# A two-layer hybrid decoder step on Trainium2: the layer loop written out, the layer's ends run token tile by token tile, and a fourth place for expert weights

## The reference

```python
def decoder_layer(x, ...):
    h = rmsnorm(x, norm1_g)
    au, av, bq, bk, bv, cq, ck, cv, cz, cb, ca = split_cols(h @ w_in)
    out_a = chunk_mlp(au, av, ...)                     # spatial gating, 4 groups x 64
    out_b = dilated_attention_blocked(q, k_all, v_all) # 6 heads, cache of 2048 rows
    qkv, conv_state = short_conv(concat(cq, ck, cv), conv_buf, c_conv_w)
    o, s_new = gated_delta(...)                        # 6 heads, chunks of 64
    x = x + concat(out_a, out_b, out_c) @ w_out
    x = x + hier_moe(rmsnorm(x, norm2_g), w_group, w_router, w1, w3, w2)
    return x, (k_new, v_new, a_rows, conv_state, s_new)
for l in range(2): xp, xs = decoder_layer(...)         # prompt and sample
y_prompt, y_sample = rmsnorm(xp, final_g), rmsnorm(xs, final_g)
```

## Time and profile before

| what | value |
|---|---|
| median of three executions | 1950.37 us |
| profiled execution, its time | 1945.06 us |
| its span, first to last instruction | 1943.1 us |
| mean granted TensorE clock | 0.883 of full |
| PE busy | 1553.9 us (80%) |
| PEld busy | 1020.3 us (53%) |
| DVE / ACT / POOL busy | 621.2 / 400.6 / 169.7 us |
| read from HBM, written | 313.25 MB, 37.83 MB |
| weights of the experts, transfers | 192 of 1024 KB, median 18.5 us from issue to landing |

### The profile page before, as it was taken

The page is one execution under the profiler, slowest core; times in us unless marked ns, Lnnn a source line. Parts: engine busy times, 40 slices in busy tenths (PEclk is TensorE's granted clock), DMA queues, the critical chain, the costliest instruction groups (busy, mean ns, idle before and its releaser), DMA issues. The chain is left out here.

```text
span 1943.1 us, 31857 instructions
## 1 busy us (share of the span) xinstructions
PE 1553.9 (80%) x12956; PEld 1020.3 (53%) x12956; DVE 621.2 (32%) x1587; ACT 400.6 (21%) x955; POOL 169.7 (9%) x211
## 2 busy tenths in 40 slices
PE   6999978887679597878399998888785896978880
PEld 3476566765445354544155765667653454544450
DVE  2433155665113211111245322566541132111113
ACT  3221122322311111111131212223232110111111
POOL 0000000000000322222000000000000012222210
PEclk9999998895789699999799989889867897999995
DMA  7152010002862599999440511000047535999984
GB/s 274 45 177 80 1 36 2 2 18 58 226 236 79 170 390 394 397 395 401 151 143 10 189 58 35 2 2 2 20 121 223 197 124 216 387 398 394 397 336 155
DMA packets 97141, 337.13 MB, mean 174 GB/s; under 512 B 33325, under 2 KB 44941, under 8 KB 72317
## 3 DMA queue, kind: packets, MB, share of 16 engines
q1 hardware_dynamic: 77484, 307.86, 44.0%
q0 software_dynamic: 13296, 25.98, 3.9%
q10 hardware_dynamic: 6240, 1.57, 0.4%
HBM read 313.25 MB, written 37.83 MB: 181 GB/s over the span
## 5 line engine op out<-in xcount | busy, mean ns | idle before, releaser
L1587 PE MATMUL bank<-ring,proj_raw 128*64 128x256 f32 x2048 | 264.2, 411 | 79.9 <-DMA ring<-in_w 77.0
L1587 PEld LDWEIGHTS bank<-ring,proj_raw 128*64 128x64 f32 x2048 | 168.8, 143 | 156.2 <-issue 94.9
L1362 PE MATMUL bank<-ring,hT_raw 128*128 128x384 f32 (+2 forms) x768 | 229.2, 462 | 0.0
L1362 PEld LDWEIGHTS bank<-ring,hT_raw 128*128 128x128 f32 x768 | 149.0, 195 | 78.0 <-issue 4.8
L2175 DVE TENSOR_TENSOR qkv_raw<-qkv_raw,bank 128x128 f32<-128x128 f32 x64 | 18.4, 287 | 446.9 <-ACT qkv_raw L1022 446.9
L1299 PE MATMUL bank<-hT_raw,ring 128*128 128x512 f32 x288 | 127.6, 596 | 0.0
L1608 PE MATMUL bank<-ring,proj_raw 128*64 128x512 f32 x512 | 123.9, 604 | 1.5 <-issue 1.5
L1507 PE MATMUL bank<-ring,hT_raw 128*128 128x512 f32 x256 | 113.6, 597 | 0.0
L1080 PE MATMUL bank<-work 64*64 64x64 f32 (+1 forms) x1608 | 73.1, 256 | 37.6 <-DVE work L1730 26.2
L1574 PE MATMUL bank<-consts,proj_raw 64*128 64x64 f32 x512 | 70.1, 278 | 29.0 <-DMA proj_raw<-h_rows,idx 29.0
L1080 PEld LDWEIGHTS bank<-work 64*64 64x64 f32 (+1 forms) x1608 | 66.7, 168 | 47.0 <-DVE work L1730 29.5
(11 more groups left out here) (312 smaller groups left out, 1988.8 us busy)
## 6 DMA issues: line engine op xcount, KB each, us to landing
ring<-in_w SPq DMA_DIRECT2D x192, 1024.0 KB, 18.5
ring<-in_w_in SPq DMA_DIRECT2D x10, 1536.0 KB, 15.1
ring<-in_cache_win_k SPq DMA_DIRECT2D x16, 768.0 KB, 8.7
ring<-in_cache_win_v SPq DMA_DIRECT2D x16, 768.0 KB, 13.7
ring<-in_cache_win_k SPq DMA_DIRECT2D x16, 576.0 KB, 6.9
ring<-in_cache_win_v SPq DMA_DIRECT2D x16, 576.0 KB, 11.1
ring<-in_w_out SPq DMA_DIRECT2D x4, 2048.0 KB, 11.7
h_rows<-proj_raw SPq DMA_DIRECT2D x16, 512.0 KB, 3.6
```

Of the source, the lines that this page charges most:

```text
L1362: mm = pe.matmul(bank[0:ROWS[t], 0:w.shape[2]], hT[:, k, 128 * t:128 * t + ROWS[t]], w[:, k, :], start=k == 0, stop=k == KT - 1)
L1587: mm = pe.matmul(bank[CAP * j:CAP * j + CAP, 0:256].rearrange("p (w f) -> p w f", w=2), rowsT[k % 2][:, CAP * c:CAP * c + CAP], w13[:, :, ...
```

## The change

The loop over layers becomes plain code, twice. Semaphores are no longer cleared: each layer has its own set (`class Signals`), or the count goes on from layer to layer. The meeting of the engines at a layer's end goes. TensorE, before it enters the second layer, waits only for the banks of the experts.

Expert weights get a fourth place, in columns of `work` and of the projection buffer `proj_raw` that hold nothing any more once the output projection begins. Expert 1 takes it, then every fourth; the ring's slots go to experts 0, 2, 3 and every fourth after each. Its first load waits for `mix_ready` and for the end of `mixT` instead of for a part of `w_out`, and stands ahead of the first four `h2_store` pairs. The expert loops of TensorE, ScalarE and VectorE take twelve experts a turn, two turns, with eight experts written out; SP's takes four.

At the ends, adding the results, the squares, the root, the scaling and (after layer 1) the final multiplication run tile by tile in a pipeline, `enter`, over ScalarE and VectorE. The next layer's gain and loads 1 and 2 are issued when `down` of experts 28 and 30 is done; load 0 is issued behind the ten reads of `y_rows`; conv state and taps behind that, when the first tile has been added (they go to columns that `got` uses). `final_g` is loaded behind the last expert's weights. The outputs are stored tile by tile. `hst` moves to the end of `qkv_raw`.

```diff
-        hst = [qkv_raw[:, D * i:D * i + D] for i in range(2)]
+        hst = [qkv_raw[:, D * (3 + i):D * (3 + i) + D] for i in range(2)]
-        EUN = 6
+        EUN = 12
+        def up_home(e):
+            slot = (E_AT, None, E_AT + 1, E_AT + 2)[e % 4]
+            return work[:, 0:4096] if slot is None else ring[:, slot % 3 * SLOT:slot % 3 * SLOT + 4096]
+        def down_home(e):
+            slot = (E_AT, None, E_AT + 1, E_AT + 2)[e % 4]
+            return proj_raw[:, 8192:10240] if slot is None else ring[:, slot % 3 * SLOT + 4096:slot % 3 * SLOT + 6144]
 # SP
-            with sp.Fori(0, DEPTH) as L:
+            gain_load(0)
+            conv_loads(0)
+            for n in range(3):
+                stream(0, n, loads[n](0, n))
+            for L in range(DEPTH):
...
-                for e in range(3):
-                    sp.wait_ge(*used_up(E_AT + e - 3))
-                    up_load(e, (E_AT + e) % 3)
-                    down_load(e, (E_AT + e) % 3)
-                    for i in ((0, 1, 2, 3), (), (4,))[e]:
+                for e in range(4):
+                    if e == 1:
+                        sp.wait_ge(s.mix_ready, 1)
+                    else:
+                        sp.wait_ge(*used_up(E_AT + (0, None, 1, 2)[e] - 3))
+                    up_load(e, e)
+                    if e == 1:
+                        sp.wait_ge(s.act_filled, A_AT[("mixT", NT - 1, 1)] + 1)
+                        sp.wait_ge(pool_stored, (L + 1) * (16 * STORES))
+                    down_load(e, e)
+                    for i in ((), (0, 1, 2, 3), (), (4,))[e]:
                         h2_store(i)
...
+                if L + 1 < DEPTH:
+                    gain_load(L + 1)
+                    for n, e in ((1, NE - 4), (2, NE - 2)):
+                        sp.wait_ge(s.act_filled, A0 + 2 * e + 2)
+                        stream(L + 1, n, loads[n](L + 1, n))
+                else:
+                    sp.dma_start(g_final, ins["final_g"][None, :].broadcast_to([128, D])).then_inc(fin_gain, 16)
...
-                leave_layer(sp, L)
+                if L + 1 < DEPTH:
+                    stream(L + 1, 0, loads[0](L + 1, 0))
+                    sp.wait_ge(got_used, L * NT + 1)
+                    conv_loads(L + 1)
+            for t in range(NT):
+                sp.wait_ge(fin_row, t + 1)
+                if t < NP:
+                    sp.dma_start(outs["y_prompt"].rearrange("b (t p) d -> t p (b d)", p=128)[t], x[:, t, :]).then_inc(y_stored, 16)
+                else:
...
 # ScalarE
+            def enter(L):
+                for t in range(NT + 1):
+                    if t < NT:
+                        if L:
+                            act.wait_ge(got_used, (L - 1) * NT + t + 1)
...
+                        act.activation(junk1[0:ROWS[t]], x[0:ROWS[t], t, :], ACT.Square, accum_out=ssq[0:ROWS[t], t:t + 1]).then_inc(row_squared, 1)
+                    if t >= 1:
+                        u = t - 1
+                        act.wait_ge(row_asked, L * NT + u + 1)
+                        act.activation(rstd[:, u:u + 1], rstd[:, u:u + 1], ACT.Sqrt).then_inc(row_root, 1)
+                        if L < DEPTH:
...
+                            act.activation(hst[u % 2][0:ROWS[u]], x[0:ROWS[u], u, :], ACT.Copy,
+                                           scale=rstd[0:ROWS[u], u:u + 1]).then_inc(of_layer[L].rows_ready, 1)
 # VectorE (joined: the two additions of tile t; asked_root: mean, EPS, reciprocal)
+            def enter(L, normed):
+                for t in range(NT + 2):
+                    if L and t < NT:
+                        joined(L - 1, t)
+                    if 1 <= t <= NT:
+                        asked_root(L, t - 1)
+                    if t >= 2:
+                        normed(t - 2)
```

More of the change, by code:

```diff
@@ L495, in build @@
+        of_layer = [Signals(L) for L in range(DEPTH)]
         a_jobs, v_jobs = schedule()
@@ L721, in _ @@
-                sp.sem_inc(aside, 1)
+                    sp.wait_ge(rows_stored[k], 16 * (L + 1) * per_buffer[k] + 16)
                 for t in range(NT):
@@ L840, in _ @@
+            for L in range(DEPTH):
+                s = of_layer[L]
+                steps, roots, asked = [0], [0], [0]
+                enter(L)
                 bank = get(("tapsT",))
-                act.activation(taps, bank[:, 0:NCT * 28].rearrange("p (c n) -> p c n", c=NCT), ACT.Copy).then_inc(act_drained, 1)
+                act.activation(taps, bank[:, 0:NCT * 28].rearrange("p (c n) -> p c n", c=NCT), ACT.Copy).then_inc(s.act_drained, 1)
                 for i in range(NCT + 1):
@@ L1261, in _ @@
             pe.wait_ge(consts_loaded, 16)
-            with pe.Fori(0, DEPTH) as L:
-                pe.wait_ge(taps_loaded, 32)
+            for L in range(DEPTH):
+                s = of_layer[L]
+                if L:
+                    pe.wait_ge(of_layer[L - 1].act_drained, A0 + 2 * NE)
+                    pe.wait_ge(of_layer[L - 1].vec_drained, V0 + 2 * NE)
+                pe.wait_ge(taps_loaded, L * 32 + 32)
                 bank, done = job(("tapsT",))
@@ L1405, in _ @@
                 for t in range(NT):
-                    delta_tile(pe, L, t, job, after, tr, lambda point, t=t: side(t, point) if t < NP else None)
+                    delta_tile(pe, s, t, job, after, tr, lambda point, t=t: side(t, point) if t < NP else None)
                 def cached(n, b):
@@ new lines, in inv_root, with step_done, joined @@
+                dve.wait_ge(s.root_ready, roots[0])
+            def step_done(ins):
+                counted[0] += 1
+                ins.then_inc(row_step, 1)
+                dve.wait_ge(row_step, counted[0])
+            def joined(L, t):
+                r = ROWS[t]
+                for k in range(2):
+                    j = 2 * t + k
+                    dve.wait_ge(gathered[j], L * 16 + 16)
+                    w = (w0, w1_)[k][0:r, place(t):place(t) + 1]
+                    ins = dve.scalar_tensor_tensor(x[0:r, t, :], got[j][0:r, :], w, x[0:r, t, :], ALU.mult, ALU.add)
+                    if k == 0:
+                        step_done(ins)
+                    else:
+                        ins.then_inc(got_used, 1)
@@ L1927, in _ @@
             groups = ((128, slice(0, NP), NP), (NS, slice(NP, NT), 1))
-            with dve.Fori(0, DEPTH) as L:
-                dve.wait_ge(first_squares, NT)
-                norm_scale()
-                dve.sem_inc(norm_asked, 1)
-                dve.wait_ge(gain_loaded, 16)
+            for L in range(DEPTH):
+                s = of_layer[L]
+                steps, roots = [0], [0]
                 def gained(label, t, h, gain):
```

752 lines of the change are left out of this document (355 added, 397 removed).

## The result

The changed kernel takes 1923.82 us (median of four executions, 1920.01 to 1926.24), the kernel before on the same chip 1951.08 us (1949.14 to 1954.27). The ratio is 0.986 with a 95% interval of 0.984 to 0.989: faster, by 27 us or 1.4%, where 26 us were predicted. On a second chip the same pair gave 1916.25 against 1948.15, ratio 0.984 (0.979 to 0.989).

The account below looks back on a forecast made before the run. The expert stage was taken to be bound by weight transfers at 390 GB/s. Terms of -16.2, -11, 0 and +1 summed to -26.2 us, taking the median from 1950.4 to 1924; range 1911 to 1938, with about 2 in 10 outside.

Parts of the forecast that it names:

- A: Expert stages: the fourth place leaves 28 experts' weights to load after `up(0)`; -16.2 us for both layers, bounds 0 and -18.
- C: End of the program: tile-by-tile work hides under the reads and the stores get smaller; -11 us, bounds -7 and -13.
- B: Layer 0 to layer 1: earlier `tapsT` wins 1.5 us, TensorE's lower clock may lose 3; 0 us, bounds -8 and +6.
- S: Start of the program: squares and single roots now stand between ScalarE's copies; +1 us, bounds -2 and +3.
- R2: Layer boundary: taps land early and TensorE keeps its clock, so B gives -8 us; 1916 us, chance 17%.
- The rest: Constants for loop counters, some `aside` increments gone, longer expert turns: 0 us, bounds -3 and +1.
- R1: Expert stages: the fourth place gives no time, leaving 1940 us; chance 8%.
- R3: Expert loops: instruction fetches of the longer turns stall TensorE; priced at +45 us, 1995 us, chance 5%.
- R4: Prefetch or pipeline waits for a semaphore reached only at the old place; A and C halve, 1937 us, chance 2%.

Follow-up runs that it names:

- run 2: Changed kernel with conv state and taps loaded into columns of `work`, issued before the reads of `y_rows`: 1910.06 us, 0.983 of the kernel before.
- run 9: Changed kernel with VectorE making all ten additions of layer 1 before the gained tiles, loads unaltered: 1910.46 us, 0.982 of the kernel before.
- run 11: Changed kernel with taps issued before the reads and all ten additions ahead of the gained tiles in layer 1: 1905.94 us, 0.981 of the kernel before.
- run 8: The changed kernel itself, unaltered, once more on a second chip: 1916.25 us, 0.984 of the kernel before.
- run 1: Changed kernel with the fourth place for expert weights taken back, leaving three places: 1933.33 us, 0.994 of the kernel before.
- run 6: Changed kernel with all 32 experts written out straight on TensorE, ScalarE and VectorE, no loop: 1913.62 us, 0.983 of the kernel before.
- no prefetch: Changed kernel with loads 1 and 2 of layer 1 issued with load 0, behind the reads and ahead of the taps: 1924.66 us, 0.989 of the kernel before.

## Why the prediction was right

The four terms that were named sum to -26.2 us, and their stages in the two profiles to -25.0: A -16.05, C -12.0, B +2.9, S +0.2. B took 2.9 us more than predicted and C and S together 1.8 less, so a part of the closeness is luck.

**A, -16.2: held.** The two stages gave -8.90 and -7.15, together -16.05. The signs came as named: `up(4)` at the end of `up(0)`, share 1.00, the first wait for weights four experts later than before in each layer (the eighth to the twelfth, the ninth to the thirteenth). Taking the place away alone gave back 14.6.

**C, -11: held, a little low.** From the last `down` to the end the kernel gained 12.0, although the reads went out 1.9 us late; from the first addition to the end it is 22.85 us, 13.6 less. The sum had been counted from the first addition, so it is this 13.6 that answers to the -11, and it lies just outside the bound of -13. The term that was off is VectorE's sum: 22.9 us from the first addition to its end were predicted and 20.4 measured. Additions (13.0) and multiplications (6.25) were as read; root requests and waits were put at 3.9 us and took 1.1. The 2.5 us for the last store were right (2.4).

**B, 0: right in its verdict, incomplete in its terms.** Predicted were -1.5 from the taps and up to +3 from the clock; measured is +2.9 up to the convolution, without the clock, whose cost falls behind that point. `tapsT` came 21.3 us behind the reads' issue and not 18.2. The order in the queue was as predicted, but the transfers ahead of the taps were slower: load 0 was counted in at 17.2 us behind the reads' issue, at 373 GB/s, and landed after 20.7, with 324 GB/s between 943 and 962 us. In all nine profiles in which the taps stand behind the reads, `tapsT` starts 0.3 to 1.1 us behind the landing of the last `w_in` load ahead of them. From `tapsT` to the convolution it took 16.15 us for 17. That leaves reads to convolution at +0.75. The clock cost what was allowed for: the convolution's first group 1.3 us, and 2.3 until the fourth load is issued (25.7 us behind the convolution's start for 23.4). With these 2.3 us B comes to +5.2, near its bound of +6. Not in the sum, only in its upper bound, was the last scatter behind loads 1 and 2: +2.2 us.

The step's reason was the queue: the taps stand last in it. That is true, and run 2 shows it. But I took the additions behind the first gain as given, and they are half of the same wait: whichever of the two is moved, 8 us come back (runs 2 and 9), and moving both gives 13 (run 11); R2 had allowed 8 for the whole.

**S, +1: right until the convolution (+0.2 and +0.5), without the clock.** I priced the half clock at the second layer's start and not here, where the same order brings it in seven profiles of ten, for 1.1 to 2.7 us by the fourth load (run 8).

**The rest, 0.** The stages between convolution and experts hold the same instructions in every version, and they took between 635.0 and 648.8 us in the profiles. The longest had a mean granted clock of 0.86, the shortest 0.88. In the two profiles compared they differ by 3.6 us, nearly all of it in layer 0. The half clock gives 2.6 of these; in layer 1, whose convolution began at half clock as well and was 2.3 us behind at the fourth load, nothing is left of it at the end of the stage (+0.1), and what took it back is not shown. With that, +2.9 at B, -0.8 at S and -1.0 at C, the predicted -26.2 becomes the -21.4 of the profiles. The medians differ by more, 27.3 us, and 31.9 on the second chip, since the profiled execution of before was 6 us under its median; in which stage those 6 us would lie no profile here shows.

**The rivals.** R1 falls by run 1, R3 by run 6; of the time that R2 promised nothing came in the change itself, though its 8 us were there to be had; R4 has nothing for it.

On R3 the traces show fetches rising from 3 to 7 and 12 without a stall that the `up`s' distance of 6.93 us would show. The Trainium skill (Runtime: NRT & Kernel Launch, Instruction fetch mechanics) says that code which runs on is fetched ahead and that a taken branch out of the window stalls. The trace agrees with the first; no run here shows a stall at a branch.

**What stays open.** In layer 1 nothing is prefetched, and still the reads go out 5.1 to 6.0 us behind the last `down` in ten of the profiles with the change or a part of it, but 3.86 or 3.87 in three (three places, straight, no prefetch) and 4.02 before. The 8 us from the last `down` on, first in the straight version, then in the change run again:

```profile
q0 software_dynamic: 160, 0.27, 9.5%
...
y_rows<-proj_raw,idx POOLq DMA_INDIRECT x1, 2.4
```

```profile
q8 instruction: 1, 0.02, 1.1%
...
y_rows<-proj_raw,idx POOLq DMA_INDIRECT x1, 4.0
```

The last scatter lands after 2.4 us in one and 4.0 in the other, and where it is late there is an instruction packet of 16 KB in the stretch. In layer 0 the delay is shown to come from loads 1 and 2. The Trainium skill (DMA: Bandwidth & Descriptors, Queues, rings and completion order) says that an increment of a semaphore lands only when all earlier writes of that transfer engine have, those of other queues too. Layer 0 is in line with that (6.1 us with the loads, 4.4 without). In the change load 2, issued at 933.78, lands at 942.5 by the line below, and the reads, which wait for the last scatter, go out at 942.72. In all ten profiles in which loads 1 and 2 went out after `down` of experts 28 and 30 the reads follow the landing of load 2 by 0.2 to 0.9 us. In three places, with both loads issued later, they follow that of load 1 by 1.3 us, and load 2, issued 1.4 us ahead of the last scatter, lands only 2.9 us behind the reads' issue: which of the earlier writes an increment waits for is not settled by these runs.

```profile
ring<-in_w_in SPq DMA_DIRECT2D x1, 1536.0 KB, 8.7
```

For the instruction packet in layer 1 it is only a suspicion, and a weak one: the packet could not be moved by itself, three places has one at the same point (3.4 us behind the last `down`) and no prefetch has two in the stretch, and neither is late. The cause in layer 1 stays open.

## What to carry to other kernels

Working tile by tile pays only if no early tile's step waits for something late: an in-order engine then holds all later tiles' ready work behind it. Put the work whose inputs arrive first ahead in each engine's order, and give the small loads that open a stage a place of their own ahead of the large ones. Where a stage is bound by transfers and the queue idles ahead of it, one more place for data is worth about the time of the bytes that it lets through early (8.1 us a layer by the sum, 7.2 to 8.9 measured, 6.4 and 8.2 when it was taken away).

## What was not expected of the hardware

- The issue of a small load held SP for 3.6 to 5.3 us where the reads and load 0 stood ahead of it (conv state, 949.09), against 0.3 to 1.0 us before the change and where it went out ahead of the reads, and three loads of 1.57 MB held it for 10.7 us. It cost nothing here: the queue was still busy with load 0 when SP was free again.
- A prefetch of 3 MB that nobody waits for delayed a scatter's completion on another queue by about 2 us in layer 0 (down to reads 5.6 to 7.0 us with it, 4.35 and 4.39 without).
- The same instructions, 640 us of them, vary by up to 14 us from profile to profile (the longest at a mean granted clock of 0.86, the shortest at 0.88). Differences of less than about 5 us are better read from the distance between two events than from the total.
